# Two orders changed in an fp32 two-block kernel: modulation rows ahead of their columns, and other work around the first expert rows

## The reference

```python
mod = adaln_params(c, w_mod[layer], b_mod[layer])          # silu(c) @ w_mod + b_mod: six rows of 1024
mod_c = adaln_params(c_ctx[None, :], w_mod[layer], b_mod[layer])
h = modulate(x, norm1_g[layer], mod[:, 0], mod[:, 1])      # rms_norm(x, g) * (1 + scale) + shift
hc = modulate(ctx, norm1_g[layer], mod_c[:, 0], mod_c[:, 1])
rq, rk, rv, rg, dq, dk, dv = jnp.split(h @ w_in[layer], IN_SPLITS, axis=-1)
...
x = x + mod[:, 2] * (jnp.concatenate([ret_lat, diff_lat], axis=-1) @ w_out[layer])
h2 = modulate(x, norm2_g[layer], mod[:, 3], mod[:, 4])
x = x + mod[:, 5] * peer_ffn(h2, ...)
```

```python
s = jnp.einsum('thpc,hpnc->thpn', q, sub_keys)             # 8 heads, 2 halves, 128 keys
best, pos = lax.top_k(cand, PEER_TOPK)                      # 16 experts of 128 * 128 for each head
gate = jax.nn.softmax(best, axis=-1)
u, vsel = expert_u[experts], expert_v[experts]
act = jax.nn.gelu(jnp.einsum('thkd,td->thk', u, hb), approximate=False)
return jnp.einsum('thk,thkd->td', gate * act, vsel)
```

## Time and profile before

| | us |
|---|---|
| median of 3 runs | 1727.83 |
| lowest, highest | 1727.57, 1728.28 |
| profiled execution | 1727.59 |
| its span | 1725.8 |
| PE busy | 1522.8 (88% of the span) |
| DVE, ACT, POOL busy | 752.1, 502.5, 290.8 |
| DMA moved | 586.8 MB, mean 340 GB/s |

### The profile page before, as it was taken

How to read it: one execution, slowest core, us unless ns; L and a number is a source line. 1 busy time by engine, 2 the same in 40 slices (tenths; PEclk the granted TensorE clock), 3 DMA queues, 4 the chain that set the end, 5 groups by cost and what they waited for, 6 DMA issues and landing times.

```text
span 1725.8 us, 15582 instructions
## 1 busy us (share of the span) xinstructions
PE 1522.8 (88%) x5474; PEld 729.0 (42%) x5474; DVE 752.1 (44%) x1816; ACT 502.5 (29%) x1284; POOL 290.8 (17%) x264
## 2 busy tenths in 40 slices
PE   7999998695479895897999887899999999999998
PEld 3444463462144541333343333343344444455443
DVE  3753167966786566456334346532312100031101
ACT  3411224332433223324434224433411110122210
POOL 0000003433433343222222213321000000000000
PEclk9999998897589897898999998899999999999999
DMA  9645438999999999999999999999886677855775
GB/s 372 216 159 196 170 110 347 420 421 421 421 395 421 421 421 420 410 421 421 417 422 420 421 421 421 412 421 422 346 302 242 249 296 283 314 212 220 291 297 187
DMA packets 93869, 586.83 MB, mean 340 GB/s; under 512 B 6880, under 2 KB 7008, under 8 KB 28128
## 3 DMA queue, kind: packets, MB, share of 16 engines
q1 hardware_dynamic: 55920, 313.19, 46.4%
q0 software_dynamic: 37440, 270.55, 38.0%
q10 hardware_dynamic: 432, 2.10, 0.3%
HBM read 584.76 MB, written 1.05 MB: 339 GB/s over the span
## 4 chain that ended last, share of the span: by engine, by line
PE 70%; DMA 19%; DVE 6%; issue 2%; ACT 2%; POOL 0%; SPq 0%; POOLq 0%; DVEq 0%; ACTq 0%
PE bank L999 34%; DMA arena<-in_peer_rows,pidx 10%; PE bank L1077 7%; DMA ring<-in_weights 7%; PE bank L691 7%; PE bank L1160 5%; PE bank L964 2%; PE bank L769 2%; DVE arena L2132 2%; PE bank L975 2%; PE bank L1006 2%; PE bank L746 2%; DMA spare<-in_peer_rows,pidx 1%; PE bank L1059 1%; PE bank L661 1%
## 5 line engine op out<-in xcount | busy, mean ns | idle before, releaser
L1634 POOL DMA_INDIRECT arena<-in_peer_rows,pidx x227 | 255.6, 1126 | 582.3 <-PE bank L1160 533.9
L2132 DVE SCALAR_TENSOR_TENSOR arena<-arena,ring 128x1024 f32<-128x1024 f32 x227 | 273.3, 1223 | 111.7 <-DMA arena<-in_peer_rows,pidx 109.2
L999 PE MATMUL bank<-ring,arena 128*128 128x512 f32 x736 | 319.4, 593 | 0.0
L999 PE MATMUL bank<-ring,hT_all 128*128 128x512 f32 x544 | 244.5, 605 | 16.3 <-issue 10.6
L1160 PE MATMUL bank<-arena,keep 128*32 128x512 f32 x908 | 159.8, 702 | 103.3 <-ACT keep L1593 103.2
L999 PEld LDWEIGHTS bank<-ring,arena 128*128 128x128 f32 x736 | 138.5, 190 | 168.8 <-issue 168.7
L999 PEld LDWEIGHTS bank<-ring,hT_all 128*128 128x128 f32 x544 | 102.8, 193 | 151.6 <-issue 141.1
L1580 ACT ACTIVATE pf<-pf 128x2 f32<-128x2 f32 x128 | 25.9, 202 | 400.0 <-DVE arena L2132 366.5
L2253 DVE TENSOR_TENSOR x_all<-x_all,bank 128x512 f32<-128x512 f32 x40 | 27.5, 688 | 209.0 <-PE bank L1077 115.1
L1160 PEld LDWEIGHTS bank<-arena,keep 128*32 128x32 f32 x908 | 21.2, 115 | 171.5 <-ACT keep L1593 134.7
L691 PE MATMUL bank<-ring,hT_all 128*128 128x512 f32 x192 | 84.3, 594 | 0.6 <-DVE hT_all L1712 0.6
(11 more groups left out here) (389 smaller groups left out, 1701.1 us busy)
## 6 DMA issues: line engine op xcount, KB each, us to landing
ring<-in_weights SPq DMA_DIRECT2D x122, 2048.0 KB
ring<-in_w_mod SPq DMA_DIRECT2D x12, 2048.0 KB
ring<-in_w_in SPq DMA_DIRECT2D x6, 2048.0 KB
ring<-in_weights SPq DMA_DIRECT2D x8, 1024.0 KB
ring<-in_weights SPq DMA_DIRECT2D x8, 512.0 KB
arena<-in_peer_rows,pidx POOLq DMA_INDIRECT x227, 15.4
mem_all<-in_b_mod POOLq DMA_DIRECT2D x3, 512.0 KB, 7.0
hT_all<-in_xT ACTq DMA_DIRECT2D x1, 1024.0 KB, 6.2
```

The source lines that it names most:

```text
L999: m = mm(b[:, :], src[:, k], slot8[w][:, k], start=(k == 0), stop=(k == KC - 1))
L1634: nc.gpsimd.indirect_dma_start(out=row_in[n % SLOTS], out_offset=None, in_=a["peer_rows"], in_offset=bass.IndirectOffsetOnAxis(ap=pidx[:, ...
L2132: stt(uslot[n % SLOTS], uslot[n % SLOTS], 1.0, h2g[n % 4], ALU.mult, ALU.mult, accum_out=pact2[:, 16 * (g % 2) + k:16 * (g % 2) + k + 1]). ...
```

## The change

It has two parts.

In the first phase PE does twelve unread products of 128 columns ahead of the sums of squares; `mod_rows(2)` follows `mod_rows(0)` directly, both `mod_columns` come behind, and the two unread 512-column products between them are gone. DVE copies piece 0 between the reciprocal and the multiply of `normed`. On DVE and ACT the copies of pieces 1 and 3, `mod_half(1)` and the scalings of half 1 stand ahead of the small chain.

Around the first rows `repeat_tokens(0, 0)` stands ahead of a transpose, the other three groups ahead of the transposes `mr1` and `md1`; ACT copies group 0 earlier and does `mix_turn("mr", 1)` behind picks 0 and 1. `out 0` moves from ahead of pick 2 to ahead of pick 4, `out 1` and `query q02` to ahead of pick 6, `regroup 1` to ahead of pick 8. On DVE the choice of the second group (`half_top(1, ...)` to `select(1)`) starts one pair of dots later.

```diff
-PICK_WORK = {2: ["out 0"], 4: ["out 1"], 6: ["regroup 1", "query q02"], 8: ["keys 02", "query q03"], 10: ["keys 03"], 16: ["h2_turns 1"],
+PICK_WORK = {4: ["out 0"], 6: ["out 1", "query q02"], 8: ["regroup 1", "keys 02", "query q03"], 10: ["keys 03"], 16: ["h2_turns 1"],
...
-                   ("A", "s12a s12b q01"), ("D", "gfirst"), ("A", "s13a s13b"), ("D", "k01 g0"),
-                   ("A", "e00a e00b e01a e01b e02a e02b e03a e03b")):
+                   ("A", "s12a s12b q01"), ("D", "gfirst"), ("A", "s13a s13b"), ("D", "k01"), ("A", "e00a e00b"), ("D", "g0"),
+                   ("A", "e01a e01b e02a e02b e03a e03b")):
...
             pe.wait_ge(sem("ones_set"), 1)
+            for _ in range(12):
+                mm(M[0][:, 0:P], ones, ones, start=True, stop=True)
             feature_sums("nx", squares_x, sem("squares_x"), ones)
             keep_warm(1)
...
             mod_rows(0, cpad)
-            keep_warm(2)
+            mod_rows(2, cpad)
             mod_columns(0)
-            mod_rows(2, cpad)
             mod_columns(2)
             keep_warm(1)
...
             diff_values(1, 1)
+            repeat_tokens(0, 0)
             diff_turn(1, 3)
             diff_values(1, 2)
             regroup(0)
             diff_values(1, 3)
-            repeat_tokens(0, 0)
             repeat_tokens(0, 1)
+            repeat_tokens(0, 2)
+            repeat_tokens(0, 3)
             pe.wait_ge(sem("mix_ret"), 2)
             turn_blocks(turn("mr1"), [PR[:, 1, c * P:(c + 1) * P] for c in range(4)])
             pe.wait_ge(sem("mix_diff"), 2)
             turn_blocks(turn("md1"), [PR[:, 1, 2048 + c * P:2048 + (c + 1) * P] for c in range(4)])
-            repeat_tokens(0, 2)
-            repeat_tokens(0, 3)
...
+            on_mod(1)
+            on_mod(3)
+            act.wait_ge(sem("mod_cols"), 2)
+            scale_input(1, 0)
+            scale_input(1, 1)
+
             act.wait_ge(sem("lg_abs"), 1)
             f(lgt, lgt, ACT.Exp, scale=-1.0).then_inc(sem("lg_exp"), 1)
...
             out_root(2)
+            repeat_copy(0, 0)
             out_squares(3, M[1], (diff_out, 8))
             out_root(3)
-            repeat_copy(0, 0)
             repeat_copy(0, 1)
-            mix_turn("mr", 1)
...
-            after = {2: [lambda: gate_exp(1)], 6: [lambda: query_copy("q02", ("k00",))], 8: [lambda: h2_square(1), lambda: query_copy("q03", ("k01",))], 10: [lambda: h2_root(1)],
+            after = {0: [lambda: mix_turn("mr", 1)], 4: [lambda: gate_exp(1)], 6: [lambda: query_copy("q02", ("k00",))], 8: [lambda: h2_square(1), lambda: query_copy("q03", ("k01",))], 10: [lambda: h2_root(1)],
...
                 link(nc.vector.reciprocal(v, v))
+                if k == 0:
+                    on_mod(0)
                 tt(dst, dst, v.unsqueeze(1).to_broadcast([P, KC, TOK]), ALU.mult).then_inc(sem("input_normed"), 1)
...
             scale_input(0, 1)
+            on_mod(1)
+            on_mod(3)
+            mod_half(1)
+            scale_input(1, 0)
+            scale_input(1, 1)
             link(ts(gd, cols[:, C_DN:C_DN + 4], 1.0 - LAM_INIT, None, ALU.mult))
...
             dve.wait_ge(sem("lg_done"), 1)
-
-            on_mod(1)
-            on_mod(3)
-            mod_half(1)
-            scale_input(1, 0)
-            scale_input(1, 1)
...
-            first = [[lambda: mix_turn("md", 1), lambda: half_top(1, 0), lambda: half_top(1, 1)], [lambda: best_pairs(1), lambda: next_pairs(1)],
-                     [lambda: pair_rows(1, 0), lambda: pair_rows(1, 1), lambda: spread(1)], [lambda: residual_out(1), lambda: select(1)], [], [lambda: h2_mean(1), lambda: key_copy(0, 2), lambda: half_top(2, 0), lambda: half_top(2, 1)],
+            first = [[lambda: mix_turn("md", 1)], [lambda: half_top(1, 0), lambda: half_top(1, 1)], [lambda: best_pairs(1), lambda: next_pairs(1)],
+                     [lambda: pair_rows(1, 0), lambda: pair_rows(1, 1), lambda: spread(1)], [lambda: residual_out(1), lambda: select(1)], [lambda: h2_mean(1), lambda: key_copy(0, 2), lambda: half_top(2, 0), lambda: half_top(2, 1)],
```

More of the change, by code:

```diff
@@ L1250, in _ @@
             f(cosb, cosb, ACT.Sin).then_inc(sem("sines"), 1)
-            on_mod(1)
-            on_mod(3)
-            act.wait_ge(sem("mod_cols"), 2)
-            scale_input(1, 0)
-            scale_input(1, 1)
             def by_tile(v):
@@ L1690, in _ @@
             normed(0, rs_x, hT)
-            on_mod(0)
             bm = cols[:, C_BM:C_BM + 16].unsqueeze(2)
```

## The result

| | before | after |
|---|---|---|
| time, median of 6 runs each | 1727.32 us | 1733.46 us |
| profiled execution, its span | 1727.59, 1725.8 us | 1736.64, 1734.8 us |
| granted clock, mean of the span | 0.942 | 0.933 |

The ratio is 1.0041, with an interval of 1.003 to 1.0051: **slower by 6 to 7 us** (5 to 9 by the interval). I had forecast 5.6 faster, and the time lies outside the range. The profiled execution of after was the slowest of its six, 3.2 us above their median, so positions in it are read beside those of the experiments.

A forecast was written before the change was run, and what follows sets the result against it. Bound by TensorE's dependent chain to some 300 us, DMA to 1245, then TensorE's work. Forecast: 1727.6 - 3.8 (first phase) - 1.6 (first rows) = 1722.2 us; own range 1720.4 to 1724.4, wider range 1718.5 to 1727.0.

The forecast's parts named there:

- the rows' part: Around the first expert rows: regain 3.8 us of idle DMA, lose 2.0 to later requests; net 1.8, taken as 1.6.
- signs of being wrong: Half clock in the first 60 us, c3x0 later than 65, or requests 16 and later over 4 us behind.
- the second modulation piece covers it: Ahead of mod_rows(2): products may end the sums 3 us earlier, but the piece lands at 17.0, so costed at nothing.
- the clock falls where the unread products stood: Rival, first phase: two low-clock spells cost 3.4 us, 0.5 of it hidden, giving 1725.1; chance 0.18.
- The rest of the front: First 67 us: projection 3.8 us earlier, columns 5.5 earlier; decay chain makes c3x0 wait 1.4, 4.0 stay, 3.8 taken.
- So 2.1 MB takes 10 us and q02 waits some 2.5 us.: Ahead of q02: queued weights and rows each get half the DMA rate, so q02 waits some 2.5 us.
- VectorE's select(1) waits for it.: Behind q02, select(1) waits for regroup 1: 306.2 instead of 302.05, so the rows behind come about 2 us later.
- The 3.8 us of idle DMA.: Requests 9 to 12 out by 285 us close the 12 us stretch at DMA share 0.68; upper end 3.8 us regained.
- an idle DMA microsecond is paid in full: Premise for 258 to 1245 us, where DMA sets the pace: each idle DMA microsecond counts fully in the time.
- The slower rival: q02's wait lowers the clock, both queries take 7.4 us each, rows lose 5.6: 1729.4; decides from 7.6 us lateness; chance 0.07.

The follow-up runs named there:

- e2: The change's second part alone (order around the first rows), with the first 60 us as in the kernel before: 1732.50 us, ratio 1.0034.
- e1: The change's first-phase part alone, twelve products included, with the order around the first rows as in the kernel before: 1726.42 us, ratio 0.9997.
- e11: The whole change without its twelve unread products: 1729.73 us, ratio 1.0016 to the kernel before.
- e3: As e1 but without the twelve unread products: 1724.58 us, ratio 0.9982 to the kernel before.
- e9: As e1 but with 20 unread products in place of twelve: 1726.34 us, ratio 0.9995 to the kernel before.
- e5: As e1 plus six unread 512-column products between mod_rows(0) and mod_rows(2): 1726.13 us, ratio 0.9992 to the kernel before.
- e10: As e9 plus six unread 512-column products between mod_rows(0) and mod_rows(2): 1725.15 us, ratio 0.9985 to the kernel before.
- e13: The kernel before with only TensorE's new first-phase order, without the twelve products and with the old copies: 1723.66 us, ratio 0.9979.
- e4: As e2 but with regroup 1 put back ahead of query q02: 1733.19 us, ratio 1.0038 to the kernel before.
- e6: As e2 but with the old places of out 0, out 1, regroup 1 and q02, and VectorE's old choice: 1726.12 us, ratio 0.9995 to before.
- e14: As e2 but with q02 two steps later, keys and q03 behind it, VectorE's group 2 selection one step later: 1727.16 us, ratio 1.0001 to before.
- e8: The first-phase part of e3 together with the order around the first rows of e6: 1722.37 us, ratio 0.9962 to the kernel before.
- e15: As e8 but with q02 one step later, keys and q03 too: 1722.66 us, ratio 0.9976 to the kernel before.
- e7: As e2 but with q02 one step later, behind picks 6 and 7, keys and q03 too: 1729.41 us, ratio 1.0016 to the kernel before.

## Why the prediction was wrong

The time came out 11.3 us above the 1722.2 of the forecast. Some 7 of them are the rows' part (1.6 less forecast, 5.4 more measured in e2) and 3.1 the front (3.8 less forecast, 0.7 less in e1). Four steps failed; the second and the third, both about q02, are the larger loss. All three of the prediction's signs of being wrong came in the profile after: a granted clock of half in the first 60 us, c3x0 at 67.08, and the 17th request at 314.79, 6.1 us behind before.

**The twelve products, costed at nothing, because "the second modulation piece covers it".** This is the first step that failed. The landing is right (17.0 forecast, 17.8 to 18.2 in the profiles with an idle engine there), and so is what the products do to the sums. But I counted the cover as free. Being early made a wait of 3.24 us, and the products cost some 4 us in the whole change (e11) and 1.8 in the front alone (e3, intervals overlapping), with a lower mean granted clock both times. The mechanism is less sure than the cost. In the three profiles with the wait (after, e1, e9) the clock from 17 to 32 us is 0.54, 0.89 and 0.66, and the two longest spells of all are among them (13.7 us in after, 10.2 in e9). But 0.89 also stands in e3, e5, e10 and e13, without the long wait, and in e4 and e6, whose first 60 us are those of before; e14, with that front too, has 0.77; the other seven profiles have 1.00. So a spell can come in any of these orders, and the wait goes with the long ones.

The rival "the clock falls where the unread products stood" had its spell at the right place: the first projection took 5.40 us in e3 and 5.37 in e13, where the two unread products are gone and no idle time over 0.73 us stands in front. But e8, e11 and e15 leave them out as well and have none, and the wait for piece 3 covered it in e3. The loss was not that. The Trainium skill (TensorE: Matmul & The Clock Gate, Why this matters for your kernels) asks for no long idle gaps between bursts. The long spells of after and e9 agree, behind 3.24 us; the profile of e1 shows that such a gap need not cost more than a shorter one.

**The rest of the front, 3.8 us.** Mechanism right, size right in places and smaller in time. Without the products the first projection starts at 23.35 (22.95 forecast), the columns at 42.7, c3x0 at 63.5, the 31st request is 3.7 us earlier, and the time falls by 2.5 us (the interval is 1.6 to 4.7), so 3.8 is not excluded. The decay chain behind the copies took back 1.7 us where I had 1.4.

**"So 2.1 MB takes 10 us and q02 waits some 2.5 us."** The second step that failed, mis-sized. Half the rate and the 10 us were right (47.6% of the engines for the weights from 294 to 298 us, 10.2 us of moving; the Trainium skill, DMA: Bandwidth & Descriptors, Queues, rings and completion order, agrees that an engine alternates between queues with work), but the piece landed 13.7 us after its request, since the rows already queued went first for 3.4 us. The wait was 5.65. The 2.5 was also a slip in my own sum: "out 0" at 290.8, the 1.0 us of picks 4 and 5 and 7.1 of "out 1" give 298.9, not 298, and so 1.9. Two terms were missing behind it: q02 itself ran at the low clock, 6.35 us instead of 3.78, and "out 0" ended at 291.5 instead of 290.8.

**"VectorE's select(1) waits for it."** The third step, and with the second the main loss: the wrong gate. The requests hang on the slot that picks 6 and 7 free. e4 moved select(1) to 299.3 us and gained nothing.

**The 3.8 us of idle DMA.** The fourth step. They did come back from 282 to 294 us, and were lost again from 306 on: from 258 to 354 us the windows of before and after have shares below full worth 5.8 us in all before and 9.7 after (each stretch by what its share lacks). Where the requests are hardly late (e14) or early (e6), the medians are 0.2 above and 0.3 below before, not 3.8 below; that this is because weights and rows now share the engines is argued from the queues' rows, and no run shows it alone. Nor is my premise borne out that an idle DMA microsecond is paid in full: the windows of e6 from 258 to 354 us lack 2.9 us against the 5.8 of before, and its time is 0.3 us lower, at most 2.4 by the interval, as far as one profile can be set beside a median. The slower rival was the right one in kind (q02's wait, the low clock behind it, deciding "from a lateness of 7.6 us on"; the 31st request was 9.0 us late in after and 6.6 in e2). I gave it 0.07, against it that "before, the picks' own products fill such waits"; here they stood behind the waiting query and could fill nothing.

## What to carry to other kernels

Idle DMA time just ahead of a weight load is not free to take: before it is filled with other requests, look who gets his data quickly because of it, and what stands behind that reader in its engine's order. Of a wait that becomes longer, list everything behind it on the engine and what each item releases; the item that frees a buffer counts for more than the one that computes the next index. An engine made faster ahead of a transfer that lands at a fixed time has only gained a wait, and on TensorE a spell of low clock can follow that is longer than the wait (13.7 us behind 3.24 in the profile after).

## What the runs showed that I had not expected

The length of a low-clock spell differs from one execution to the next behind the same wait: after a wait of 3.24 us the projection of 3.67 us took 5.53, 5.40 and 5.58 us, but the clock of the window from 17 to 32 us was 0.54, 0.89 and 0.66. Nor does such a spell need the wait: with the front of before it was 1.00 in before, e2 and e7, 0.89 in e4 and e6 and 0.77 in e14. The mean granted clock of all executions tells more about a cause than one profile. A single profile may thus be 3 us from its kernel's median.

The same 2 MB weight piece landed 14 us after its request in e14, 13.7 in after, and in at most 9.3 before; what differed were the rows queued around it.

The first request of e1 was 1.9 us earlier than before and its 31st 5.0, yet its span was only 1.5 us shorter (1724.3 against 1725.8). At 1237 us the lead was 2.3 us, and the output projection there took 7.86 us instead of 7.13: a lead won early can be paid back later on, and one request's place is no measure of the time.
